# Stick-breaking attention and paged decode on one core: steps cut into three equal slots, decode units placed slot by slot

## The reference, cut to what matters

```python
def stick_breaking(q, k, v, sb_bias, q_pos, k_pos):
    z = jnp.einsum('bqhd,bkhd->bhqk', q, k) * (HEAD_DIM_SB ** -0.5) + sb_bias[None, :, None, None]
    mask = k_pos[None, :] < q_pos[:, None]
    log_1mb = jnp.where(mask, jax.nn.log_sigmoid(-z), 0.0)
    suffix = lax.cumsum(log_1mb, axis=3, reverse=True) - log_1mb
    a = jnp.where(mask, jnp.exp(jax.nn.log_sigmoid(z) + suffix), 0.0)
    return jnp.einsum('bhqk,bkhd->bqhd', a, v)
# prompt: 8 heads x 64, 2048 queries x 2048 keys, causal
# decode: k_past = cache_k[page_table], v_past = cache_v[page_table]; 128 pages of 128 tokens each of k and of v
```

## Time and profile before

| | us |
|---|---|
| median of 3 runs | 3199.69 (3199.49 to 3204.03) |
| the profiled execution: its own time | 3203.6 |
| its span | 3202.0 |
| of it `attend`, from its first instruction to the next part's | 551 to 1247 |
| PE, DVE, ACT, POOL busy over the span | 3057.1, 2031.6, 1632.7, 147.3 |

### The profile page before, as it was taken

One profiled execution on the slowest core, in us unless ns is written; L12 is line 12 of the kernel. 1 busy time (PEld: TensorE's weight loads), 2 busy tenths in 40 slices (PEclk: granted clock), 3 DMA queues, 4 the chain that ended last, 5 costly groups with the idle time before them and its releaser, 6 DMA issues.

```text
span 3202.0 us, 51792 instructions
## 1 busy us (share of the span) xinstructions
PE 3057.1 (95%) x18572; PEld 2825.0 (88%) x18572; DVE 2031.6 (63%) x2725; ACT 1632.7 (51%) x2359; POOL 147.3 (5%) x277
## 2 busy tenths in 40 slices
PE   8999998888699878999999999999999999999998
PEld 6888887777377747999999999999999999999998
DVE  4222443868577867776577756777567774778845
ACT  5444312988488866444445444455344443444433
POOL 0000000111312130000000000000000000000000
PEclk9999999999799989999999999999999999999999
DMA  5234456554845564443354343643336334443342
GB/s 182 92 103 135 127 151 178 135 146 108 233 123 147 129 180 134 134 118 112 108 166 139 112 116 107 185 122 116 111 113 184 113 115 116 143 132 114 113 117 77
DMA packets 599824, 422.81 MB, mean 132 GB/s; under 512 B 38842, under 2 KB 564067, under 8 KB 596931
## 3 DMA queue, kind: packets, MB, share of 16 engines
q1 hardware_dynamic: 558596, 318.23, 35.6%
q0 software_dynamic: 20544, 67.19, 7.2%
q10 hardware_dynamic: 20512, 35.17, 3.1%
HBM read 367.26 MB, written 53.25 MB: 131 GB/s over the span
## 4 chain that ended last, share of the span: by engine, by line
PE 61%; DVE 0%; issue 0%; DVEq 0%; ACT 0%; ACTq 0%
PE pf_acc L60 20%; PE pf_acc L58 20%; PE pf_acc L59 20%; PE pf_ps_t L1696 1%; PE pf_ps_sum L1635 0%; PE pf_ps_sum L1644 0%; PE pf_ps_sum L1649 0%; PE pf_ps_t L1706 0%; PE pf_ps_t L1767 0%; DVE late_ssum L1974 0%; DVE late_u L1964 0%; DVEq L1572 0%; DVE late_c L2042 0%; DVE pf_h L2168 0%; ACT late_sq L1795 0%
## 5 line engine op out<-in xcount | busy, mean ns | idle before, releaser
L1788 ACT ACTIVATE late_w_hi<-ahead_raw 128x1024 fp32r<-128x1024 f32 x439 | 463.8, 1057 | 551.3 <-PE pf_acc L60 547.4
L60 PE MATMUL pf_acc<-pf_x_hi,late_w_lo 128*128 128x416 f32 x2080 | 734.1, 353 | 0.0
L58 PE MATMUL pf_acc<-pf_x_hi,late_w_hi 128*128 128x416 f32 x2080 | 733.1, 352 | 0.0
L59 PE MATMUL pf_acc<-pf_x_lo,late_w_hi 128*128 128x416 f32 x2080 | 726.0, 349 | 0.0
L1958 DVE TENSOR_TENSOR late_w_lo<-ahead_raw,late_w_hi 128x1024 fp32r<-128x1024 f32 x439 | 536.4, 1222 | 269.8 <-ACT late_w_hi L1788 269.0
L58 PE MATMUL pf_acc<-late_f_hi,late_w_hi 128*128 128x416 f32 x1280 | 453.7, 354 | 6.8 <-DVEq L2181 6.8
L60 PE MATMUL pf_acc<-late_f_hi,late_w_lo 128*128 128x416 f32 x1280 | 452.4, 353 | 0.0
L59 PE MATMUL pf_acc<-late_f_lo,late_w_hi 128*128 128x416 f32 x1280 | 447.8, 350 | 0.0
L59 PEld LDWEIGHTS pf_acc<-pf_x_lo,late_w_hi 128*128 128x128 f32 x2080 | 390.8, 188 | 7.9 <-issue 1.6
L58 PEld LDWEIGHTS pf_acc<-pf_x_hi,late_w_hi 128*128 128x128 f32 x2080 | 390.5, 188 | 3.7 <-issue 1.6
L60 PEld LDWEIGHTS pf_acc<-pf_x_hi,late_w_lo 128*128 128x128 f32 x2080 | 390.0, 187 | 2.3
(11 more groups left out here) (238 smaller groups left out, 4025.1 us busy)
## 6 DMA issues: line engine op xcount, KB each, us to landing
ahead_raw<-in_w_up_dram SPq DMA_DIRECT2D x220, 512.0 KB, 3.9
ahead_raw<-in_w_down_dram SPq DMA_DIRECT2D x80, 512.0 KB, 4.0
high_pages<-in_cache_k_dram POOLq DMA_DIRECT2D x128, 256.0 KB, 3.6
ahead_raw<-in_w_out_dram SPq DMA_DIRECT2D x40, 512.0 KB, 5.6
ahead_raw<-in_w_ple_gate_dram SPq DMA_DIRECT2D x40, 512.0 KB, 4.1
high_pages<-in_cache_v_dram POOLq DMA_DIRECT2D x64, 256.0 KB, 3.3
at_kT<-in_cache_v_dram POOLq DMA_DIRECT2D x64, 256.0 KB, 3.3
ahead_raw<-in_w_down_dram SPq DMA_DIRECT2D x40, 384.0 KB, 3.4
```

Source lines behind the costliest of these rows:

```text
L58: nc.tensor.matmul(out, stat_hi, mov_hi, start=first, stop=False)
L59: nc.tensor.matmul(out, stat_hi, mov_lo, start=False, stop=False)
L60: return nc.tensor.matmul(out, stat_lo, mov_hi, start=False, stop=last)
L1788: nc.scalar.activation(w_hi[k % 4][:, :], raw[k % 4][:, :], ACT.Copy).then_inc(hi_split, 1)
```

## The change: what it does

Every step has three slots of equal form, and units are placed in slots. Slot `g` of step `t` holds, on TensorE: the turned fills of the decode units of that slot, a part of the product with v, the products of the units of the slot before, the prompt's turns (two runs in slot 0, one in slot 1, two in slot 2), and the logits of granule `g`. ScalarE follows in the same order, so it now copies a unit's product in the slot of the product, not a step later.

- The pair product with v stands in five parts over two steps: tiles 0 to 3, 4 to 7 and 8 to 10, then 11 to 13 and 14 to 16.
- The planner has a pace: a key unit every 1.5 slots (two each step, in slots 0 and 1), a sum every 1.875 slots. Keys of group 0 start in step 0 (before: 3) and take steps 0 to 15; its sums stand in steps 20 to 30, its mix in step 31 (product in 32). Group 1: keys in 32 to 47, sums in 52 to 62, mix in 63 (product in 64).
- `stage` has three buffers.
- VectorE makes the masks and the first queries in step 0, before its first scan (before: in step 1).

```diff
+    SLOTS, END = GRANULES, STEPS + LAG + 2
+    TURNS = (0, 1), (2,), (3, 4)
+    WEIGHED = ((0, 4), (4, 8), (8, 11)), ((11, 14), (14, 17), (17, 17))
...
-            if apart(u) and units_of[t]:
-                t += 2 if u in (U_TURN, U_MIX) else 1
-            while t < last_unit and (t + 1 - first_unit) * GROUPS * UNITS < placed * (last_unit - first_unit):
-                t += 1
-            units_of[t].append((g, u))
...
+    KEY_PACE, SUM_PACE = 1.5, 1.875
...
+            pace = max(pace, earliest(g, u, at_slot))
+            at_slot[g, u] = int(pace)
+            pace += KEY_PACE if u < KEY_UNITS else SUM_PACE if U_SUM <= u < U_MIX else 0
...
+    def turned_units(t, g):
+        return [unit for unit, n in at_slot.items() if n == SLOTS * t + g]
+
+    def product_units(t, g):
+        return [unit for unit, n in at_slot.items() if n + 1 == SLOTS * t + g]
...
+    def weighed(s, g):
+
+        if s == STEPS:
+            return range(TILES if g == 0 else 0)
+        return range(*WEIGHED[s % 2][g]) if 2 <= s < STEPS else range(0)
...
-        own, stage = beta_s[:, 0:BANK], [beta_s[:, (n + 1) * BANK:(n + 2) * BANK] for n in range(2)]
+        own, stage = beta_s[:, 0:BANK], [beta_s[:, (n + 1) * BANK:(n + 2) * BANK] for n in range(3)]
...
+                    for g in range(SLOTS):
+                        for unit in turned_units(t, g):
+                            sample_turns(*unit)
+                        weigh(s - 2 - s % 2, weighed(s, g))
+                        for unit in product_units(t, g):
+                            sample_products(*unit)
+                        if has(s) and g == 0:
+                            pe.wait_ge(a_done, s + 1)
+                        for r in turns(t, g):
                             turn(s, r)
-                        if has(t) and g < GRANULES:
+                        if has(t):
                             logits(t, g)
-                    if has(s - 2) and s % 2 == 0:
-                        weigh_pair(s - 2)
...
+                    for g in range(SLOTS):
+                        for unit in turned_units(t, g):
+                            sample_copies(*unit)
+                        if weighed(s, g) and weighed(s, g)[-1] == TILES - 1:
+                            pair_out((s - 2) // 2)
+                        for unit in product_units(t, g):
+                            sample_sigmoids(*unit)
+                        for r in turns(t, g):
                             take(s, r)
...
-                        if n >= 2:
-                            act.wait_ge(summed, n - 1)
+                        if n >= 3:
+                            act.wait_ge(summed, n - 2)
...
-                    if t == 1:
+                    if t == 0:
                         dve.wait_ge(masks, 1)
                         sample_masks()
```

More of the change, by code:

```diff
@@ L912, in run_tiles, with earliest @@
         return range(4 * r, min(4 * r + 4, TILES))
[L914 to L922, removed]
+    KEY_PACE, SUM_PACE = 1.5, 1.875
+    def earliest(g, u, at):
+        if u == 0:
+            return at[g - 1, U_MIX] + 1 if g else 0
+        if u < KEY_UNITS:
+            return at[g, u - 1] + (2 if u % 4 == 0 else 0)
+        if u == U_WEIGHT:
+            return 3 * (at[g, U_SCAN] // 3 + 1)
+        if u == U_TURN:
+            return 3 * (at[g, U_WEIGHT] // 3 + 2)
+        if u == U_MIX:
+            return 3 * ((at[g, U_MIX - 1] + 1) // 3 + 2) - 1
+        return at[g, u - 1] + (4 if u == U_SCAN else 1)
@@ L946, in product_fills @@
             if u < KEY_UNITS and u % 4 == 3:
-                fills.append(("z", g, u // 4))
+                fills.append(("z", group, u // 4))
             if u == U_NEW:
-                fills.append(("new", g))
+                fills.append(("new", group))
             if U_SUM <= u < U_MIX:
-                fills.append(("sum", g, u - U_SUM))
+                fills.append(("sum", group, u - U_SUM))
             if u == U_MIX:
-                fills.append(("mix", g))
+                fills.append(("mix", group))
@@ L954, in product_fills, with turns @@
         return fills
[L956 to L963, removed]
-    order = []
[L966 to L969, removed]
-            order += [("turn", s, r) for r in range(RUNS)]
-        order += product_fills(t)
+    def turns(t, g):
+        return TURNS[g] if has(t - LAG) else ()
@@ L972, in attend @@
+    def weighed(s, g):
+        if s == STEPS:
+            return range(TILES if g == 0 else 0)
+        return range(*WEIGHED[s % 2][g]) if 2 <= s < STEPS else range(0)
+    order = []
+    for t in range(END):
+        for g in range(SLOTS):
+            order += turned_fills(t, g) + product_fills(t, g) + [("turn", t - LAG, r) for r in turns(t, g)]
     fill_at = {key: n for n, key in enumerate(order)}
@@ L1294, in _ @@
                             .then_inc(join["early_sum"], 1)
-                    for g, u in units_of[t]:
-                        sample_products(g, u)
             @block.scalar
```

75 lines of the change are left out of this document (33 added, 42 removed).

## The result

The changed kernel takes 3121.4 us, the median of four runs (3120.0 to 3122.4), against 3201.8 for the kernel before beside it (3199.5 to 3204.0). The ratio is 0.9749, 95% interval 0.9732 to 0.9765: 80 us faster. 3109 was forecast, with a range of 3084 to 3146. The profiled execution took 3120.0 us, with a span of 3118.4; against the profiled one of before, 83.6 less, where the prediction had 90.9.

The account below looks back on a forecast made before the run. In `attend`, sums waited for pages and PE and ACT for each other in key steps; PE is full behind it. 578.4 + 126.1 + 133 + 155.2 + 133 + 20 = 1145.7; 3199.7 - 90.9 = 3109 us, range 3084 to 3146.

Parts of the forecast that it names:

- mark of step 3: Start of step 3 in `attend`: 570.6 plus 4.8 for ten more key copies and 3 for late pages, 578.4 us.
- given back at the end: After the last product: the last chain starts behind the product, costing 1.5 us with the semaphore.
- Key steps: Steps 3 to 15 and 32 to 47: 9.7 us each, between 9.2 and 10.1; 126.1 and 155.2 us.
- without the alternation by 1 us: Sign of being right: key steps take 9.4 to 10.0 us, no longer alternating by 1 us.
- Sum steps: Steps 16 to 31 and 48 to 63: VectorE late last with 136.4 us of work; 133 us each, up to 141.
- VectorE without idle time there: Sign of being right: VectorE has no idle time in steps 20 to 31.
- Pages late: Rival, 12%: a head's load still delays the sums' pages, at steps 28 and 52; +22 us, 3131.
- The end: From step 64 to the last product's end: VectorE's lag shows, 20 us.
- The third buffer: Sum steps: a third stage buffer lets ACT run while VectorE is a step late; with two it would wait.
- Half clock: Rival, 12%: PE's clock falls in steps without keys, four such steps a group at +3.6 us; +29 us, 3138.
- Lockstep: Rival, 5%: PE and ACT take turns in steps 3 to 66, losing 1.2 us a slot; slower, 3266.
- Nothing in the key steps: Rival, 10%: key steps stay at 10.1 us, both engines being full; +12 us, 3121.

Follow-up runs that it names:

- the first two experiments: Kernel before with only the new unit table: 3165.0 us; changed kernel with the product with v in one piece, in a pair's second step: 3147.1 us.
- the new table alone: Kernel before with only the changed kernel's unit table, read by steps; steps, whole product and two stage buffers as before: 3165.0 us, ratio 0.9889.

## Why the prediction was right, and where it was off

The main mechanism was right: once the sums are spread, their pages are there but for one in each group, and the sum stretches fall to the size that was forecast. The change was forecast at 91 us and gave 80. The total is nearer than its terms: key steps and late pages came out 14.5 us over, and an end that was put 7.3 us too long hid half of that, which is luck. The marks, predicted and measured:

| term | predicted | measured |
|---|---|---|
| mark of step 3 | 578.4 | 578.5 |
| steps 3 to 15 | 126.1 | 129.3 |
| steps 16 to 31 | 133 | 135.7 |
| steps 32 to 47 | 155.2 | 158.5 |
| step 48 to the end of the last product | 153 | 149.9 |
| of that, mark of step 63 to the end of the last product | 28.3 | 21.0 |
| end of the last product | 1145.7 | 1152.0 |
| given back at the end | 1.5 | 1.3 |

**Key steps**, a term that was mis-sized: 9.7 predicted, 9.94 and 9.91 measured, 6.5 us in 29 steps. The cut was put at 0.1 us a step. TensorE's busy time grew by 19.22 - 18.87 = 0.35 a pair, 0.17 a step. ScalarE's wait of about 1 us a pair was named rightly (1.06) but it is not what sets the pair. TensorE is: 0.96 us less on it took 0.87 off a pair, and ScalarE's wait all but gone took nothing. TensorE's 19.2 and its one wait of 0.7 are the 19.93. Moving tiles between the steps does not change this sum. The sign "without the alternation by 1 us" failed: the steps alternate between 10.9 and 9.1.

**Sum steps**: the size of 133 us was right where no page is late: 132.7 for steps 16 to 31 with the early head loads. The reason was wrong. I had VectorE late last, at 136.4 us of work; with 0.6 us less in each addition no step moved, and with TensorE relieved they fell. Its lag was also misread: the prediction has 58 us of its work in steps 20 to 25, where its own row has VectorE busy 45.90 of 50.90 us and its list of terms without sums comes to some 53. Two engines at 131 and 134 of 136 look alike in the windows, and the sign "VectorE without idle time there" came true (134.24 of 135.70) without deciding anything; only taking work from each told which one is the bound.

**Pages late**, a rival at 12% and +22 us, held in part, elsewhere. I looked for it at steps 28 and 52; it came at steps 23 and 55, 3 and 5 us over a step of 9.2, behind the loads that SyncE issues at steps 20 and 52. Moving these removed both, and 8.0 us with them in the traces, 11 in the medians. Between 1145.7 and 1152.0 stand, then, the mark of step 3 (+0.1), the key steps (+6.5), the late pages (+8.0), 1.0 less in the rest of the sum stretches, and the end (-7.3).

**The end** was sized by VectorE's lag, and that was wrong too. From the mark of step 63 to the last product's end it took 21.0 us, not 8.3 + 20. It took the same 21.0 in the kernel before (1217.15 to 1238.14), which the prediction could have read off, and the same 21.0 with less work on VectorE in the sums, where its last weights start 1 us earlier: its lag did not set this stretch.

With 1.3 us more behind the reciprocal (1956.5 against 1955.2) and 0.2 less given back that is the 7.3 us between 90.9 and 83.6. The other 5 us between 3109 and 3121.4 are how the profiled executions lie to their medians: before's was 3.9 over the one that the forecast used, after's is 1.5 under.

**The third buffer** does what was said, ScalarE runs on while VectorE is late, but its 7 us were hidden behind the late pages until these were gone.

**Half clock** (12%) did not come: 1.00, 1.00, 1.00 and 0.99 in the four stretches, 0.88 in step 55 alone, which has the wait of 3.3 us. The page of the Trainium skill that was weighed ("TensorE: Matmul & The Clock Gate", "A second HAM failure mode: psum-queue depth-cycling") reports for a bf16 kernel that the clock swings when banks are cycled with small idle times between groups of matmuls; the trace does not show it here, the stretches cycle through three banks with products cut in five, with a wait of 0.7 us in 20, and stay at full clock. **Lockstep** (5%) did not come either: TensorE was busy 58.00 of 58.00 us from 785 to 843 and 19.22 of 19.93 in a key pair. POOL's pace stayed at 1.16 us with VectorE busy 17.77 of 18.16:

```profile
745.61:763.77 18.16, 18.16 (x178) 13.18 (x176) 17.77 (x19) 17.17 (x29) 8.60 (x16) 1.00 1.03 214
```

The Trainium skill ("Advanced Engine Details and Errata", "GPSIMD Details") says that POOL conflicts with VectorE's instructions with two SBUF inputs, by which its issues would come slower here; the trace does not agree.

**Nothing in the key steps** (10%, 3121) has the measured time, but by luck: the key steps were at 9.9, between it and the forecast, and the late pages did the rest.

What stays open: why the mark of step 3 differs between kernels with the same slots there (577.9 to 581.2 us; the pages of the first key steps are fetched then, beside the load of a head, but no run separates the two), how much of the 18 us between the first two experiments is the third buffer, and what packed sums cost without a head load beside them.

## What to carry to other kernels

When work waits for transfers that one engine issues at a fixed pace, spread it to that pace; here this gave nearly half of the gain by itself, and packing it again lost 40 us, part of them to the head loads that the packed sums met. A table that balances one resource can pile up another: the new table alone made key steps 0.6 us longer, and the finer slots and the cut brought the other half of the gain. Where two engines are both over 95% busy, take work from each in turn before saying which is the bound, and ask what a big load that shares the DMA does to small ones that are due at the same time.

## What the runs showed of the hardware that I had not expected

A page of 256 KB landed in 3.2 us (median) with 0.5 MB of a head load beside it and in 15.8 when 3.5 MB had begun to be issued 4 us before the first page; moving 3 MB of it by four steps was enough, and so was a lead of 9 us. Cutting a run of matmuls in pieces cost TensorE between 0.07 us a cut (0.13 busy us less for two cuts fewer) and 0.15 (the starts of the five parts). The share of a step in which TensorE is busy does not tell its clock: with the new table alone a step of 10.60 us with 8.24 busy was granted 0.84, and a step of 9.10 us with 6.76 busy 1.00. In the first TensorE had two waits for ScalarE's copies, 0.81 and 1.23 us, with 0.63 us of work between them, and in the second 1.05 and 1.23:

```profile
613.60:624.20 10.60, 8.24 (x50) 7.10 (x50) 5.67 (x3) 9.18 (x16) 3.23 (x6) 0.84 0.55 148
636.70:645.80 9.10, 6.76 (x50) 5.48 (x49) 6.03 (x3) 8.90 (x17) 2.69 (x5) 1.00 0.50 140
```
